# Thirty-two bytes of padding ahead of the weight ring of a two-block transformer kernel

## The chip, the cores and the metric

The kernel runs on one core of one Trainium2 chip. The metric is device time in microseconds of one execution. Three runs of the kernel before took 1617.83, 1611.34 and 1613.09 us; their median is 1613.09 us.

## The reference

One sequence of 256 tokens and 1024 features goes through two blocks, in fp32.

```
first_block:   h += mix(rmsnorm(h)) @ w_out          # 8 forgetting heads, 8 stick-breaking heads
               h += cross_attention(h, mem)          # 4 heads, 256 memory rows
               h += moe(rmsnorm(h))                  # router, 16 experts of 256 hidden units
               x  = rmsnorm(h)
second_block:  for l in 0, 1:                        # also carries 256 context rows through layer 0
                 h = modulate(rmsnorm(x), ...) @ w_in
                 x += gate * (concat(fourier, mLSTM both ways, latent attention) @ w_out)
                 x += gate * (square(relu(modulate(rmsnorm(x)) @ w_up)) @ w_down)   # 4096 hidden
               return rmsnorm(x)
```

Nearly all of the arithmetic is products of an activation matrix of 256 or 512 rows with fp32 weights.

## The kernel before

Activations lie feature-major: a tile such as `res` or `uh` holds, for each block of 128 features, 256 or 512 token columns. Weights come as 350 pieces of [128, 1024] fp32 (`PIECE`), 4,096 bytes in every partition, in the order in which they are used.

The precision of fp32 is kept by splitting each operand in two parts of type fp32r. For each piece SyncE's queue starts a DMA into a slot of `ring` (L471, L479, L483), four slots in turn (`RING`). ScalarE rounds the slot into `wh` (`hi_part`, L600), VectorE writes the remainder into `wl` (`lo_part`, L1747), and TensorE multiplies. ScalarE and VectorE run three pieces ahead (`AHEAD`). A slot of `ring` may be loaded again when VectorE has written the `wl` of its former piece (semaphore `w_lo`); a slot of `wh` and `wl` may be written again when TensorE has begun the next piece (`piece_used`).

A block of 128 weights takes three matmuls, `prod` at L1124 (weights stationary, activations moving) or `prod_t` at L1131 (the other way round); all are issued at L1100:

```
mm(o, h, xh, start=start, stop=False, **flags)
mm(o, h, xl, start=False, stop=False, **flags)
return mm(o, lo, xh, start=False, stop=stop, **flags)
```

So one piece is 24 matmuls. In the names of the profile the moving operand stands first and the stationary one second: `pair<-uh,wh` moves `uh` against the weights `wh`.

The moving pairs are `uh`,`ul` (projections, output products, up products), `xh`,`xl` (queries of the cross attention), `fh`,`fl` and `hidh`,`hidl` (experts), and `hh`,`hl` (down products). In `prod_t` `wh` and `wl` move and `uh` and `ul` are stationary (values of the first block and some of the second).

Places in SBUF are given out by hand. The base is rounded up to 32 bytes and every tile is put at a running count of fp32 words:

```
base = (nc.sbuf_base + 31) // 32 * 32
return nc.alloc_sbuf_tensor_at(name, list(shape), dtype, offset=base + 4 * off)
```

Ahead of the ring `take` gives out, in words: `table` 3,976, `lw` 1,408, `res`, `uh` and `ul` 4,096 each, `sq` and the row buffers 2,560 each, `rstd` 512, `small` 256, `modv` 192, `gmod` 64, `macc` 16, `gcol` 32. That is 23,864 words or 95,456 bytes, 745 times 128 and 96 over. With a base on a multiple of 128 bytes, `table` starts at 0 past such a multiple, `lw` up to `gmod` (`uh`, `ul` and `sq` among them) at 32 past one, and `macc`, `gcol`, `ring`, `wh`, `wl`, `spin` and the common region `w0` at 96 past one. In `w0` lie, one after the other and over each other, `qk`, `kx`, `vx`, `qx`, `xh`/`xl`, `fh`/`fl`, `gates`, `eg`, `hidh`/`hidl`, `qkp`, `qc`, `mv`, `mo`, `va`, `pf`, `cq`, `ya`, `hh`/`hl` and the early buffers `qk_w` and `qk_c`. Their places count from `w0` in multiples of 16 words.

Of the kernel before, what the change touches and what calls it, by code (L numbers as in the profile page):

```python
# [228 lines left out]
def build(nc, w_stream, mod_stream, c_rows, ml_dram, gate_dram, table_in, small_in, x_in, mem_in, ctx_in, out):  # L229
    with ExitStack() as stack:  # L230
# [11 lines left out]
        def at(name, shape, off, dtype=F32):  # L242
            n = int(np.prod(shape[1:]))
            return nc.alloc_sbuf_tensor_at(name, list(shape), dtype, offset=base + 4 * off)

        def take(n):
            top[0] += n
            return top[0] - n
# [23 lines left out]
        gmod = at("gmod", [P, 2 * NL, 16], take(64))  # L272
        macc = at("macc", [P, 2 * UNIT_TURN], take(16))
        gcol = at("gcol", [P, 2, 4, MH], take(32))
        ring = at("ring", [P, RING, PIECE], take(RING * PIECE))
        wh = at("wh", [P, RING, PIECE], take(RING * PIECE), F32R)
        wl = at("wl", [P, RING, PIECE], take(RING * PIECE), F32R)
# [2442 lines left out]
```

## Time and profile before

| | |
|---|---|
| median of three runs | 1613.09 us (1611.34 to 1617.83) |
| span of the profiled execution, first to last instruction | 1611.0 us |
| TensorE, matmuls | 1552.7 us busy, 96% of the span, 9,912 of them |
| VectorE | 1068.4 us busy, 66% |
| ScalarE | 758.7 us busy, 47% |
| mean granted TensorE clock | 0.994 of 2.4 GHz |
| DMA | 254.90 MB, 158 GB/s over the span |

The profile gives the profiled execution's span; its own time is not listed apart from the three runs above. A busy matmul's end is modelled and overlaps the next one's start, so the time that a matmul costs is read from one start to the next, not from its duration.

### The profile page before, as it was taken

To read this page: it belongs to the slowest core of one execution; us is meant where nothing else is said; L and a number is where in the kernel's file an instruction comes from. 1 tells how busy PE (TensorE), PEld (TensorE's weight loads), DVE (VectorE), ACT (ScalarE), POOL (GpSimd) and SP (SyncE) were. 2 spreads that over 40 slices of the span, in tenths; PEclk is the share of its full clock that TensorE was granted. 3 is DMA by queue.
4 is the path that set the end of the run, shared out by engine and by line. 5 is a ranking of instruction groups with operands and counts; after the bars stand their busy time and mean duration, and the time that the engine had idled before them with its cause. 6 is when DMAs were issued, how large, how long until landed. Compare 5 with 4: busy or idle time off the path is not lost.

```text
span 1611.0 us, 27225 instructions
## 1 busy us (share of the span) xinstructions
PE 1552.7 (96%) x9912; PEld 1367.7 (85%) x9912; DVE 1068.4 (66%) x1834; ACT 758.7 (47%) x1302; POOL 99.7 (6%) x167
## 2 busy tenths in 40 slices
PE   7999999999999999998799999999999998999997
PEld 7998798999999987765587888888887875899997
DVE  5877586888888879516856645555577845665554
ACT  5544544544444454434634532245225355574562
POOL 0011000000000000000200100010000002000000
PEclk9999999999999999999999999999999999999999
DMA  8675172677777733320241754455453442245552
GB/s 338 220 273 193 53 240 85 211 244 244 241 242 243 227 92 110 100 66 18 62 131 63 237 179 148 143 184 196 142 161 91 127 110 40 88 153 188 174 182 91
DMA packets 71784, 254.90 MB, mean 158 GB/s; under 512 B 7920, under 2 KB 11152, under 8 KB 71456
## 3 DMA queue, kind: packets, MB, share of 16 engines
q1 hardware_dynamic: 54048, 189.43, 36.1%
q0 software_dynamic: 17664, 64.49, 13.2%
q8 instruction: 48, 0.79, 0.2%
q14 instruction: 24, 0.20, 0.0%
HBM read 252.78 MB, written 1.11 MB: 158 GB/s over the span
## 4 chain that ended last, share of the span: by engine, by line
PE 86%; DVE 8%; ACT 3%; issue 2%; DMA 0%; DVEq 0%; SPq 0%; ACTq 0%
PE pair L1100 85%; PE pair L1144 1%; DVE sq L2359 1%; ACT wh L600 1%; DVE uv L1788 1%; DVE sq L1828 1%; DVE small L1820 1%; PE pair L1289 1%; ACT sq L668 0%; DMA table<-in_table 0%; DVE wl L1747 0%; ACT rstd L637 0%; DVE ul L1777 0%; DVE res L2512 0%; ACT rstd L639 0%
## 5 line engine op out<-in xcount | busy, mean ns | idle before, releaser
L1747 DVE TENSOR_TENSOR wl<-ring,wh 128x1024 fp32r<-128x1024 f32 x350 | 426.4, 1222 | 202.4 <-ACT wh L600 198.3
L600 ACT ACTIVATE wh<-ring 128x1024 fp32r<-128x1024 f32 x350 | 366.6, 1052 | 263.9 <-PE pair L1100 245.9
L1100 PE MATMUL pair<-uh,wh 128*128 128x256 f32 (+3 forms) x1280 | 417.3, 326 | 6.8 <-DVE ul L1779 4.1
L1100 PE MATMUL pair<-uh,wl 128*128 128x256 f32 (+3 forms) x1280 | 413.1, 323 | 0.0
L1100 PE MATMUL pair<-ul,wh 128*128 128x256 f32 (+3 forms) x1280 | 412.0, 322 | 0.0
L1100 PEld LDWEIGHTS pair<-uh,wh 128*128 128x128 f32 (+1 forms) x1280 | 235.8, 184 | 32.9 <-issue 8.2
L1100 PEld LDWEIGHTS pair<-uh,wl 128*128 128x128 f32 (+1 forms) x1280 | 235.9, 184 | 23.9
L1100 PEld LDWEIGHTS pair<-ul,wh 128*128 128x128 f32 (+1 forms) x1280 | 235.7, 184 | 23.3
L1100 PE MATMUL pair<-hh,wh 128*128 128x512 f32 (+1 forms) x512 | 172.7, 337 | 0.8
L1100 PE MATMUL pair<-hh,wl 128*128 128x512 f32 (+1 forms) x512 | 172.0, 336 | 0.0
L1100 PE MATMUL pair<-hl,wh 128*128 128x512 f32 (+1 forms) x512 | 172.0, 336 | 0.0
L1100 PE MATMUL pair<-fh,wh 128*128 128x256 f32 x520 | 147.5, 284 | 1.1 <-DVE res L1975 1.1
L1100 PE MATMUL pair<-fl,wh 128*128 128x256 f32 x520 | 147.1, 283 | 0.0
L1100 PE MATMUL pair<-fh,wl 128*128 128x256 f32 x520 | 147.1, 283 | 0.0
L1100 PEld LDWEIGHTS pair<-hh,wh 128*128 128x128 f32 x512 | 97.1, 190 | 11.9 <-issue 2.0
L1100 PEld LDWEIGHTS pair<-hl,wh 128*128 128x128 f32 x512 | 97.2, 190 | 10.1
L1100 PEld LDWEIGHTS pair<-hh,wl 128*128 128x128 f32 x512 | 97.1, 190 | 10.0
L1100 PEld LDWEIGHTS pair<-fh,wh 128*128 128x128 f32 x520 | 99.8, 192 | 1.3 <-DVE res L1975 1.3
L1100 PEld LDWEIGHTS pair<-fl,wh 128*128 128x128 f32 x520 | 99.8, 192 | 0.0
L1100 PEld LDWEIGHTS pair<-fh,wl 128*128 128x128 f32 x520 | 99.8, 192 | 0.0
L2480 DVE TENSOR_TENSOR hl<-sq,hh 128x512 f32 (+1 forms) x64 | 35.7, 558 | 95.0 <-ACT hh L1059 94.9
L1054 ACT ACTIVATE sq<-pair 128x512 f32<-128x512 f32 (+1 forms) x64 | 31.3, 489 | 107.3 <-PE pair L1100 107.3
(304 smaller groups left out, 2439.3 us busy)
## 6 DMA issues: line engine op xcount, KB each, us to landing
ring<-in_w_stream SPq DMA_DIRECT2D x350, 512.0 KB, 4.2
mod_w<-in_mods POOLq DMA_DIRECT2D x48, 512.0 KB, 3.8
uh_f<-in_mods POOLq DMA_DIRECT2D x42, 512.0 KB, 5.1
qk_w<-in_mods POOLq DMA_DIRECT2D x6, 512.0 KB, 7.0
uv<-c_rows POOLq DMA_DIRECT2D x4, 512.0 KB, 7.0
ml<-ml_dram POOLq DMA_DIRECT2D x4, 512.0 KB, 7.7
table<-in_table SPq DMA_DIRECT2D x1, 1849.5 KB, 12.6
res<-in_x SPq DMA_DIRECT2D x4, 256.0 KB, 4.1
```

Source lines behind the costliest of these rows:

```text
L600: act.activation(wh[:, s, :], ring[:, s, :], ACT.Copy).then_inc(S("w_hi"), 1)
L1054: act.activation(r, bank[(b0 + j) % 4][:, 0:n], ACT.Relu).then_inc(S("job_emptied_act"), 1)
L1100: ins = pe.matmul(*operands, **flags)
L1144: pe.matmul(bank[b], spin[:, 0:P], spin[:, :], start=True, stop=True)
L1289: last = pe.transpose(bank[6][:, to * P:(to + 1) * P], prob[i % 2][:, j * P:(j + 1) * P], ident)
L1747: tt(wl[:, s, :], ring[:, s, :], wh[:, s, :].bitcast(F32), ALU.subtract).then_inc(S("w_lo"), 1)
L1788: last = stt(o, src, g, r, ALU.mult, ALU.mult)
L1820: dve.tensor_reduce(smv(i, 0, 0, g), b, AX_X, ALU.max, negate=True).then_inc(S("sm_max"), 1)
L1828: last = ts(p, p, smv(i, 1, k), None, ALU.mult)
L2359: last = stt(e[:, tc], bank[4 + kb % 2][:, tc], MD ** -0.5, e[:, tc], ALU.mult, ALU.mult)
L2480: tt(hl[:, d, 0:n].rearrange("p a b -> p (a b)"), sq[:, 2 + j % 2, 0:n], hh[:, d, 0:n].rearrange("p a b -> p (a b)").bitcast(F32), ALU.sub ...
```

## The change

One line takes eight words that nothing uses. Everything that is given out after it starts 32 bytes later; nothing else differs: the instructions, their order, their waits and their shapes are the same.

```
         gcol = at("gcol", [P, 2, 4, MH], take(32))
+        take(8)
         ring = at("ring", [P, RING, PIECE], take(RING * PIECE))
         wh = at("wh", [P, RING, PIECE], take(RING * PIECE), F32R)
         wl = at("wl", [P, RING, PIECE], take(RING * PIECE), F32R)
```

With the base as above, `ring`, `wh`, `wl`, `spin` and `w0` then start on a multiple of 128 bytes, and every tile in `w0` on a multiple of 64. `table`, `res`, `uh`, `ul`, `sq` and the others ahead of the line stay where they were.

## Rows read from the trace of the kernel before

**Rows 1.** The page: span, busy time, and the chain that ended last.
```profile
span 1611.0 us, 27225 instructions
PE 1552.7 (96%) x9912; PEld 1367.7 (85%) x9912; DVE 1068.4 (66%) x1834; ACT 758.7 (47%) x1302; POOL 99.7 (6%) x167
...
PE 86%; DVE 8%; ACT 3%; issue 2%; DMA 0%; DVEq 0%; SPq 0%; ACTq 0%
PE pair L1100 85%; PE pair L1144 1%; DVE sq L2359 1%; ACT wh L600 1%; DVE uv L1788 1%; DVE sq L1828 1%; DVE small L1820 1%; PE pair L1289 1%; ACT sq L668 0%; DMA table<-in_table 0%; DVE wl L1747 0%; ACT rstd L637 0%; DVE ul L1777 0%; DVE res L2512 0%; ACT rstd L639 0%
```

**Rows 2.** Groups of TensorE by form: names, shape, count; busy us, mean ns.
```profile
L1100 PE MATMUL pair<-uh,wh 128*128 128x256 f32 x696 | 196.6, 282 | 5.0 <-DVE ul L1779 2.2 <-DVE wl L1747 1.1 <-DVE ul L1777 1.1
...
L1100 PE MATMUL pair<-uh,wh 128*128 128x512 f32 x392 | 155.2, 396 | 1.9 <-DVE ul L1779 1.9
...
L1100 PE MATMUL pair<-fh,wh 128*128 128x256 f32 x520 | 147.5, 284 | 1.1 <-DVE res L1975 1.1
...
L1100 PE MATMUL pair<-hh,wh 128*128 128x512 f32 x256 | 99.6, 389 | 0.0
...
L1100 PE MATMUL pair<-hh,wh 128*128 128x256 f32 x256 | 73.0, 285 | 0.8
L1100 PE MATMUL pair<-hidh,wh 128*128 128x256 f32 x256 | 72.4, 283 | 0.0
...
L1100 PE MATMUL pair<-wh,uh 128*128 128x256 f32 x128 | 35.4, 277 | 0.0
```

**Rows 3.** The chain in four stretches without a wait: start us, us, matmuls.
```profile
68.99 21.08 PE pair L1100 x186
...
305.95 259.08 PE pair L1100 x2159
...
864.77 80.34 PE pair L1100 x351
...
954.96 80.24 PE pair L1100 x354
```

**Rows 4.** TensorE's timeline, two stretches: start us, us; first and last rows.
```profile
142.81 0.28 PE L1100 MATMUL pair<-wh,uh 128*128 128x256 f32 x1
...
143.98 0.28 PE L1100 MATMUL pair<-wl,uh 128*128 128x256 f32 x1
...
263.76 0.28 PE L1100 MATMUL pair<-uh,wh 128*128 128x256 f32 x1
...
266.12 0.28 PE L1100 MATMUL pair<-uh,wl 128*128 128x256 f32 x1
```

**Rows 5.** Who waited for whom: us in total, times, longest us.
```profile
ACT wh L600 <- PE pair L1100: 245.9, 113, 4.5
...
ACT wh L600 <- DMA ring<-in_w_stream: 17.8, 13, 3.3
...
PE pair L1100 <- DMA table<-in_table: 8.5, 1, 8.5
...
PE pair L1100 <- DVE wl L1747: 1.1, 2, 0.7
```

**Rows 6.** The tile `ring`: time of its DMAs from issue to landing.
```profile
DMA to landing us min/median/max: 3.4/4.2/10.6
```

**Rows 7.** Groups of VectorE and ScalarE by form: names, shapes, count; busy us, mean ns.
```profile
L1747 DVE TENSOR_TENSOR wl<-ring,wh 128x1024 fp32r<-128x1024 f32 x350 | 426.4, 1222 | 202.4 <-ACT wh L600 198.3 <-issue 3.3 <-DVE sq L2494 0.4
...
L1880 DVE CUSTOM_DVE_ANT_1 uh_f<-uh_f,uv 128x1024 f32<-128x1024 f32 x12 | 14.6, 1220 | 0.0
...
L1880 DVE CUSTOM_DVE_ANT_0 qk_w<-qk_w,qk_c 128x1024 f32<-128x1024 f32 x6 | 7.3, 1214 | 0.0
...
L2273 DVE SCALAR_TENSOR_TENSOR qc<-qkp,table,qc 96x256 f32<-96x256 f32 x16 | 7.7, 481 | 0.6
...
L1788 DVE SCALAR_TENSOR_TENSOR uv<-res,gmod,rstd 128x256 f32<-128x256 f32 x40 | 17.3, 477 | 3.8 <-ACT rstd L639 3.8
...
L600 ACT ACTIVATE wh<-ring 128x1024 fp32r<-128x1024 f32 x350 | 366.6, 1052 | 263.9 <-PE pair L1100 245.9 <-DMA ring<-in_w_stream 17.8
```

More of the change, by code:

```diff
@@ L274, in build @@
         gcol = at("gcol", [P, 2, 4, MH], take(32))
+        take(8)
         ring = at("ring", [P, RING, PIECE], take(RING * PIECE))
```

## The prediction

> **What bounds the kernel now.** I read the page first. TensorE's matmuls fill 1552.7 of 1611.0 us, and the chain that ended last runs through TensorE for 86% of the span, through VectorE for 8%, ScalarE for 3% and DMA for 0% [rows 1]. The reader should see two things there: the time is made by matmuls that follow each other without a wait, and weight loading is not on the path. The waits say the same. ScalarE's rounding of weights waited 245.9 us for TensorE and only 17.8 us for the ring's DMAs, and TensorE waited 1.1 us in all for VectorE's remainder of a piece [rows 5].
>
> So the first question of a change of addresses is whether the pace of the matmuls depends on an address. A matmul's duration in the groups (282 ns for 256 columns) overlaps the next one [rows 2], so I took the pace from unbroken stretches of the chain [rows 3] and from starts in the timeline [rows 4]:
>
> - `fh`,`fl` and `hidh`,`hidl` moving, 256 columns: 259.08 us for 2,159, or 120.0 ns each.
> - `uh`,`ul` moving, 256 columns: 20 steps from 263.76 to 266.12, or 118.0 ns.
> - `wh`,`wl` moving, `uh`,`ul` stationary, 256 columns: 21.08 us for 186, or 113.3 ns, in one stretch; 10 steps from 142.81 to 143.98, or 117 ns, in another.
> - `uh`,`ul` moving, 512 columns: 80.34 us for 351, or 228.9 ns.
> - `hh`,`hl` moving, 512 columns: 80.24 us for 354, or 226.7 ns.
>
> From 256 to 512 columns of operands behind the ring the pace grows by 226.7 - 120.0 = 106.7 ns, so the columns alone cost 106.7 ns per 256, and what lies on top is 6.7 ns (113.3), 11.3 ns (118.0) or 13.3 ns (120.0 and 226.7). These differ with the operands, and the operands differ in their place modulo 128: `uh` and `ul` at 32, everything behind the ring at 96. That is all that speaks for an effect. Against it: the same operands with the same form ran at 113.3 and at 117 ns in two stretches, at one and the same alignment. So at least part of the spread is a rhythm into which TensorE's loads and matmuls fall, not an alignment.
>
> **The change part by part.** No instruction, wait or DMA is added, removed or reordered. Four things could still cost differently.
>
> *The ring's DMAs.* 350 of them now write 32 bytes further on. A landing takes 4.2 us in the median [rows 6]. ScalarE works three pieces ahead, and a piece is 24 matmuls: 24 x 118.0 ns = 2.8 us, three are 8.5 us. A landing could take twice as long before TensorE saw it in the steady stretches. Where it doesn't hide, at the start, TensorE's longest DMA wait is for `table` (8.5 us), which does not move, and its waits for a split piece are 1.1 us [rows 5]. Bounds -1.1 and +1.1 us; I take 0.
>
> *ScalarE and VectorE.* `wl` from `ring` and `wh`, 1,024 elements at 96 past a multiple of 128, takes 1222 ns. A pass of the same size over tiles at 32 past one takes 1220 ns (`uh_f`), one over tiles at 96 takes 1214 ns (`qk_w`). The convolution reads `qkp` shifted by single words and takes 481 ns for 256 elements, against 477 ns for the unshifted `uv` [rows 7]. So a shift by four bytes costs at most 4 ns, 0.8%. These two engines hold 11% of the chain, 177 us [rows 1]; 0.8% of it is 1.4 us. Bounds -1.4 and +1.4 us; I take 0. The rest of their work is covered by TensorE: a piece costs VectorE 1222 ns and ScalarE 1052 ns [rows 7] against its 2.8 us there.
>
> *Matmuls whose two operands both move by 32 bytes.* These are `fh`,`fl` (520 each of three), `hidh`,`hidl` (256 each) and `hh`,`hl` at 256 columns (256 each): 3 x 1,032 = 3,096; and 3 x 256 = 768 of 512 columns [rows 2]. Their distance to each other stays, the place modulo 128 changes. No fp32r operand of the trace starts on a multiple of 64, so this is bounded. Lowest: nothing but the columns, 3,096 x 13.3 ns + 768 x 13.3 ns = 41.2 + 10.2 = 51.4 us saved. Highest: one more step of the size seen between 113.3 and 120.0, 6.7 ns on each: 3,864 x 6.7 ns = 25.9 us lost. I take 0, because the nearest rows, the pair at 113.3 and 117 ns at one alignment, show paces that change without it.
>
> *Matmuls of which one operand moves.* `uh`,`ul` against `wh`,`wl`: 3 x 696 = 2,088 of 256 columns, 3 x 392 = 1,176 of 512; and 3 x 128 = 384 with `wh`,`wl` moving [rows 2]. Lowest: all of 256 columns at 113.3, 2,088 x 4.7 ns = 9.8 us saved, and 1,176 x 6.7 ns = 7.9 us. Highest: 2,088 x 2.0 ns (to 120.0) + 1,176 x 6.7 ns + 384 x 6.7 ns (113.3 to 120.0) = 4.2 + 7.9 + 2.6 = 14.7 us lost. I take 0 for the same reason.
>
> The Trainium skill (Advanced Engine Details and Errata, Memory Cachelines) puts SBUF's lines at 16 bytes; 96 and 0 past a multiple of 128 are both starts of such a line, and by this rule no operand would gain or lose. It leaves the three paces unexplained, and no run here shows the size of a line.
>
> The sum is 0 on a span of 1611.0 us. The profiled execution's own time isn't listed apart; its span lies just under the fastest of the three runs (1611.34) and 2.1 us below their median of 1613.09, so I forecast 1612 us, between the two.
>
> **The rivals.**
>
> *Faster: alignment sets the extra time of a matmul (chance 0.33).* For it: operands behind the ring hold 120.0 ns over 2,159 matmuls without one slip, those at 32 hold 118.0, as if the place fixed the step; and the steps between paces are 6.7 ns, the time of 16 columns or 64 bytes, which is what a start off a multiple of 64 could cost. Against it: the two paces at one alignment. If operands that both move fall one step: 3,864 x 6.7 ns = 25.9 us, 1587 us. If the `uh` matmuls of 256 columns follow to 113.3, 9.8 us more, 1577 us. If half of the first comes, 1600 us.
>
> *Slower: the distance between `uh` and the weights decides (chance 0.21).* `uh` at 32 and `wh` at 96 were 64 bytes apart modulo 128 and become 32 apart; should weight load and moving read then meet more often, only the matmuls with one moved operand pay: 14.7 us as above, 1628 us (1620 to 1635). It decides from about 2.3 ns on each of the 3,648. For it: `uh` against `wh` is quicker than `fh` against `wh` (118.0 to 120.0), so something in the pairing counts. Against it: at 512 columns the order is the other way round (228.9 to 226.7).
>
> *The change doesn't do what it says (0.03, inside no change).* The base is only rounded to 32 bytes; if it isn't on a multiple of 128, neither is the ring after the change. That would be another place modulo 128, with the same forecast.
>
> *A quicker DMA is hidden (inside no change).* If the landings became shorter, ScalarE's 17.8 us of waiting would shrink, and the chain, which has 0% of DMA, would not.
>
> **How the numbers follow.** No change (within 0.5%, or 8 us, about what a measurement of this kernel tells from none): 0.46; faster 0.33; slower 0.21. The likeliest is 1612 us, its own range 1605 to 1620. The range for 8 in 10 takes in the one-step gain (1587) with little to spare and most of the slower case: 1585 to 1627. It leaves out the gain with `uh` following and the far end of the slower case.
>
> **What would show it.** Right: the same paces in the same stretches, 120.0 ns for `fh`, 118.0 for `uh`, 228.9 and 226.7 ns for 512 columns, `wl` at 1222 ns and `wh` at 1052 ns, landings near 4.2 us. Wrong: the stretch of 2,159 matmuls of the experts, 259.08 us long, shortens to about 245 us (113.3 ns) or lengthens; or the stretch of 351 of `uh` with 512 columns leaves 80.34 us. If the span changes and all paces stand, the cause lies in the waits between stretches, and I would have missed it.

## The result and the profile after

The changed kernel takes 1618.07 us (median of 20 runs, 1614.44 to 1621.77) against 1614.32 us (20 runs) before. The ratio is 1.0023 with a 95% interval of 1.0012 to 1.0034: 3.7 us slower, small but clear of noise. The forecast of 1612 us stood for no change, a little below the time before, and the time rose; the slower rival had named the place and overpriced it.

The page after (compare [rows 1]). TensorE's busy time grew by 8.5 us, VectorE's and ScalarE's did not, and the chain runs through TensorE as before:

```profile
span 1619.3 us, 27225 instructions
PE 1561.2 (96%) x9912; PEld 1370.4 (85%) x9912; DVE 1068.2 (66%) x1834; ACT 758.2 (47%) x1302; POOL 99.7 (6%) x167
...
PE 87%; DVE 7%; ACT 3%; issue 2%; DMA 0%; DVEq 0%; SPq 0%; ACTq 0%
```

ScalarE's and VectorE's split of a piece and the ring's landings (compare [rows 5 to 7]). The source's lines are one higher in number now. The groups, busy us and mean ns:

```profile
L1748 DVE TENSOR_TENSOR wl<-ring,wh 128x1024 fp32r<-128x1024 f32 x350 | 426.5, 1223 | 202.8 <-ACT wh L601 198.7
L601 ACT ACTIVATE wh<-ring 128x1024 fp32r<-128x1024 f32 x350 | 366.5, 1052 | 259.2 <-PE pair L1101 245.4
```

and the tile `ring`:

```profile
DMA to landing us min/median/max: 3.3/4.2/11.5
```

1223 against 1222 ns, 1052 against 1052, 4.2 us against 4.2: these three steps held. The chain's stretches (start us, us, matmuls; compare [rows 3], in the order of the stages) show what moved:

```profile
68.94 21.06 PE pair L1101 x178
...
263.95 16.10 PE pair L1101 x138
...
307.90 259.20 PE pair L1101 x2160
...
869.85 80.27 PE pair L1101 x344
...
959.87 80.24 PE pair L1101 x354
```

The reader divides. `fh` and `hidh` moving: 259.20 / 2,160 = 120.0 ns, as before. `hh` with 512 columns: 80.24 / 354 = 226.7 ns, as before. `uh` with 512 columns: 80.27 / 344 = 233.3 ns, where it was 228.9. `wh` moving against `uh`: 21.06 / 178 = 118.3 ns, where it was 113.3. `uh` with 256 columns: 16.10 / 138 = 116.7 ns, where the same stretch before (16.14 us for 137) had 117.8. Only pairs of which one operand moved have another pace.

The steps from one matmul's start to the next, averaged over all of a kind in the trace (steps over 1.12 times the median, which hold a wait, left out), give the sum:

| moving, stationary, columns | matmuls | before ns | after ns | us |
|---|---|---|---|---|
| `uh`, weights, 512 | 1,176 | 229.06 | 233.31 | +5.0 |
| `uh`, weights, 256 | 2,088 | 117.52 | 117.13 | -0.8 |
| weights, `uh`, 256 | 384 | 114.05 | 118.35 | +1.7 |
| weights, `uh`, 384 | 192 | 175.69 | 173.42 | -0.4 |
| `uh`, 96 weights, 512 and 256 | 288 each | 233.30, 113.92 | 231.71, 116.71 | +0.3 |
| `fh`, `hidh`, `xh`, `hh` | 4,056 | | within 0.1 | -0.1 |
| sum | | | | +5.7 |

The 20 runs of each kernel differ by 3.7 us, the steps by 5.7. The two profiled spans differ by 8.3 us. Most of the rest of that is the clock: the profile after has two more stretches at the 1.2 GHz level. In windows of TensorE (busy us, matmuls, granted clock, DMA share, GB/s) after:

```profile
170.00:189.00 19.00, 17.82 (x104) 1.00 0.00 1
190.00:194.00 4.00, 4.00 (x16) 0.57 0.00 0
...
787.00:791.00 4.00, 4.00 (x16) 0.59 0.08 26
```

and before in the first of these places:

```profile
190.00:194.00 4.00, 4.00 (x30) 1.00 0.00 0
```

16 matmuls in place of 30, 14 x 0.12 us = 1.6 us in the first. In the second, the same work, from 14 matmuls `mv`,`sq` to the next group but one of the same pair, took from 783.29 to 787.36 us before and from 785.78 to 791.52 us after: 4.07 and 5.74 us, 1.7 us more. With the steps' 5.7 us that is 9.0 us, 0.7 more than the spans say. The 19 us ahead of the first stretch held a TensorE busy for 17.82 us with 104 matmuls. The same window before held 17.46 us with 102, and the clock there stayed up, so these rows don't tell why it fell. Nor do the runs make the clock a trait of the change: the 20 runs of the changed kernel have a mean granted clock of 0.9946, the 35 runs of the kernel before that were timed beside the first four experiments 0.9937. At a mean granted clock of 0.998 the changed kernel took 1614.4 and 1614.8 us, at 0.992 1620.0 to 1621.8, about 1.1 us for a thousandth.

### The profile page after: what moved, and what is told of

The parts are those of the page before. It is cut to its first block, busy times and chain, and to the rows that moved or that the text cites. A ratio compares the mean times of both kernels' runs of the same rounds, so it can differ in the third digit from the quotient of the medians.

```text
span 1619.3 us, 27225 instructions
## 1 busy us (share of the span) xinstructions
PE 1561.2 (96%) x9912; PEld 1370.4 (85%) x9912; DVE 1068.2 (66%) x1834; ACT 758.2 (47%) x1302; POOL 99.7 (6%) x167
## 4 chain that ended last, share of the span: by engine, by line
PE 87%; DVE 7%; ACT 3%; issue 2%; DMA 0%; DVEq 0%; SPq 0%; ACTq 0%
PE pair L1101 85%; PE pair L1145 1%; DVE sq L2360 1%; ACT wh L601 1%; DVE uv L1789 1%; DVE sq L1829 1%; DVE small L1821 1%; PE pair L1290 1%; ACT sq L669 0%; DVE wl L1748 0%; DMA table<-in_table 0%; ACT rstd L638 0%; DVE ul L1778 0%; DVE res L2513 0%; ACT rstd L640 0%
## 5 line engine op out<-in xcount | busy, mean ns | idle before, releaser
L1748 DVE TENSOR_TENSOR wl<-ring,wh 128x1024 fp32r<-128x1024 f32 x350 | 426.5, 1223 | 202.8 <-ACT wh L601 198.7
L601 ACT ACTIVATE wh<-ring 128x1024 fp32r<-128x1024 f32 x350 | 366.5, 1052 | 259.2 <-PE pair L1101 245.4
```

Source lines behind the costliest of these rows:

```text
L601: act.activation(wh[:, s, :], ring[:, s, :], ACT.Copy).then_inc(S("w_hi"), 1)
L1748: tt(wl[:, s, :], ring[:, s, :], wh[:, s, :].bitcast(F32), ALU.subtract).then_inc(S("w_lo"), 1)
```

## The experiments

Write d for the start of the moving operand less the start of the stationary one, modulo 256 bytes. Before, `uh` on weights has d = 64, the pairs behind the ring have 0, and weights on `uh` have 192. The change makes these 32, 0 and 224. Theory after the result: d sets the pace. Main rival: the operand's own place modulo 128 does. A distance doesn't depend on the base from which all places count, so the prediction's worry about the base has no part in what follows.

**Everything 32 bytes later.** No padding at the ring:

```
+        take(8)
         table = at("table", [P, N_COLS], take((N_COLS + 7) // 8 * 8))
```

> Eight words are taken ahead of the first tile and none ahead of the ring: every tile starts 32 bytes later, the distance between any two tiles is that of the kernel before. Theory (distance between moving and stationary operand modulo 128 sets the pace): paces as before, uh moving 512 columns 229 ns, uh moving 256 columns 117.8 ns, wh moving 256 columns 113 ns, fh 120.0 ns; time within 0.1% of before. Rival A (the operand's own place modulo 128 sets the pace): weights on a multiple of 128 as in the changed kernel, so 233.3 ns for uh with 512 columns and 118.3 ns for wh moving; time about 0.2% over before.

Measured: ratio 0.9999 (0.9983 to 1.0016). The weights now lie where the changed kernel has them, and the pace of `uh` with 512 columns is that of before, 76.22 / 333 = 228.9 ns:

```profile
869.88 76.22 PE pair L1101 x333
```

`fh` stays at 120.0 and `uh` with 256 columns at 117.5 ns. Weights and `uh` have both changed their place modulo 128 and their pace is that of before, so the operand's own place falls as a cause. One detail missed: the first stretch of `wh` moving, 192 matmuls, ran at 117.8 instead of 113.4 ns; with it the mean of that kind is 116.3, not 113.

**Sixteen words instead of eight, d = 0 everywhere.**

```
+        take(16)
         ring = at("ring", [P, RING, PIECE], take(RING * PIECE))
```

> Sixteen words ahead of the ring in place of eight: ring, wh, wl and all behind start at 32 past a multiple of 128, as uh and ul do, so moving and stationary operand are at distance 0 in every matmul, as they are for fh, hidh and hh in all kernels. Theory (distance): all fp32r pairs pace as those do, 120.0 ns for 256 and 226.7 ns for 512 columns. uh with 256 columns 2,088 x +2.2 ns = +4.6 us, uh with 512 columns 1,176 x -2.3 ns = -2.7 us, wh moving 256 columns 384 x +6.6 ns = +2.5 us: in all +4 us or +0.3% over before. Rival A (own place): weights at 32 are a new place, fh and hh would leave 120.0 and 226.7 ns. Rival B (no address matters, the paces are chance): paces of before or of after come back in no order.

Measured: 1.0017 (1.0002 to 1.0032), +2.7 us where +4 were expected. `uh` with 512 columns, then `wh` moving:

```profile
867.97 80.24 PE pair L1101 x354
...
69.91 18.12 PE pair L1101 x151
```

80.24 / 354 = 226.7 and 18.12 / 151 = 120.0 ns, and `uh` with 256 columns 119.9: at d = 0 `uh` paces exactly as `fh` and `hh` do. `fh` and `hh` kept theirs, so both rivals fall: weights at a new place changed nothing for them, and the paces came in the order of d.

**Thirty-two words, the same place modulo 128.** The diff is the same with `take(32)`.

> Thirty-two words ahead of the ring: ring and all behind start 128 bytes later than before, the same place modulo 128. Theory (distance modulo 128): paces and time as before, uh 512 columns 229 ns, wh moving 256 columns 113 ns, time within 0.1% of before. Rival C (the period is 256 bytes or more, or any move of the addresses reshuffles the paces): at least one of these paces moves by 1 ns or more.

Measured: 1.0006 (0.9988 to 1.0024). The time stands, the paces don't: `uh` with 512 columns

```profile
863.81 80.27 PE pair L1101 x344
```

goes to 233.3 ns and with 256 columns to 115.2. So the period is not 128 bytes. `uh` is at d = 192 here, at 64 before. The two shifts cancel (+5.0 and -4.8 us), which is why a time alone would have said "no effect". That any move reshuffles the paces is ruled out by the first experiment.

**Only the region behind the weights 32 bytes later.**

```
+        take(8)
         w0 = take(16464)
```

> Eight words are taken ahead of the region w0 alone: ring, wh and wl stay at 96 as before, fh, hidh, xh and hh move to 0, 32 bytes ahead of the weights. Theory (distance): uh pairs stay at 229, 117.8 and 113 ns; the pairs with fh, hidh, xh and hh leave 120.0 and 226.7 ns, which no change so far has moved: if +32 does what the change did to uh at -32 bytes (or the reverse), 256 columns go to 116.7 to 118 ns and 512 columns to 229 to 233 ns: 3,288 x -2 to -3.3 ns = -6.6 to -10.9 us and 768 x +2.3 to +6.6 ns = +1.8 to +5.1 us, in all -9 to -1.5 us. Rival D (only uh and ul, ahead of the ring, are sensitive): fh and hh stay at 120.0 and 226.7 ns, time as before.

Measured: 0.9976 (0.9959 to 0.9994), -3.9 us. The first line is `fh` and `hidh`, the second `hh` with 512 columns:

```profile
309.96 240.10 PE pair L1101 x2058
...
949.91 70.23 PE pair L1101 x301
```

116.7 and 233.3 ns: the two paces that `uh` took in the changed kernel, at the same d = 32. The rival that only `uh` is sensitive falls.

These kernels also show that 256 bytes is a period. Counted modulo 512, `uh` starts 256 bytes past the weights in the kernel with sixteen words and `fh` and `hh` start level with them, and all pace alike (120.0 and 226.7 ns). `uh` is at 288 in the changed kernel and `fh` and `hh` at 32 here, and again both show 116.7 and 233.3 ns. Steps finer than 32 bytes were not tried.

**The other distances.** Four kernels with words ahead of the ring and ahead of `w0`: 48 and 32, 24 and 48, 40 and 40, 56 and 24.

> Forty-eight words ahead of the ring and thirty-two ahead of w0: uh to wh is 128 bytes modulo 256, and fh, hidh, xh, hh to wh is 128 bytes modulo 256 as well. Theory with period 128: distance 0 modulo 128 everywhere, so 120.0 ns for 256 and 226.7 ns for 512 columns for all pairs, as with sixteen words ahead of the ring; time +0.2 to +0.3% over before. Theory with period 256: a distance not seen yet, at least one of the two paces differs by 1 ns or more.

> Twenty-four words ahead of the ring and forty-eight ahead of w0: wh lies 32 bytes (modulo 128) above uh, and fh, hidh, xh, hh lie 64 bytes (modulo 128) from wh. Theory (distance modulo 128, sign indifferent): uh pairs pace as in the changed kernel, 116.7 and 233.3 ns; fh and hidh go from 120.0 to the two paces seen at 64, 113.3 or 117.8 ns, hh with 512 columns from 226.7 to 229.0 or 233.3 ns. Time: fh, hidh, xh, hh 256 columns 3,288 x -2.2 to -6.7 ns = -7 to -22 us, hh 512 columns +2 to +5 us, uh as the changed kernel +4 us: -1 to -14 us against before. Rival D (fh and hh keep what 32 bytes gave, 116.8 and 233.3 ns, at any distance but 0): 116.8 ns at 64 too.

> Forty words ahead of the ring and forty ahead of w0: uh is 96 bytes modulo 256 from wh, and fh, hidh, xh, hh 160 bytes. Theory with period 128 and sign indifferent: all pairs are 32 bytes from the weights, 116.7 ns and 233.3 ns for all. With period 256: uh or fh, at least one, paces otherwise.

> Fifty-six words ahead of the ring and twenty-four ahead of w0: uh is 160 bytes modulo 256 from wh, fh, hidh, xh, hh 96 bytes from it in the same direction as in the kernel with forty words, mirrored. Theory with period 128 and sign indifferent: the same paces as there, 116.7 ns and 233.3 ns for all pairs, and a time within 0.15% of that kernel's. If the sign counts: the paces of uh and of fh change places between the two kernels.

Measured, in that order: 1.0051 (1.0030 to 1.0072), 0.9969 (0.9952 to 0.9986), 1.0057 (1.0042 to 1.0072), 1.0092 (1.0066 to 1.0118). The chain of `fh` and `hidh` in the four, in the same order:

```profile
314.93 245.17 PE pair L1102 x2066
```
```profile
309.99 240.04 PE pair L1102 x2118
```
```profile
314.95 245.11 PE pair L1102 x2089
```
```profile
319.90 240.12 PE pair L1102 x2001
```

118.7, 113.3, 117.3 and 120.0 ns. Period 128 is refuted (120.0 was expected at 128 and 118.7 came), so is the rival that `fh` has one pace at every distance but 0 (113.3 at 192, where 32 gave 116.7), and so is an indifferent sign (32 gives 116.7, 224 gives 118.3). The last expectation was badly framed: it took the distances of `uh` and `fh` as mirrored, but by the signed d both are at 160 in the kernel with 40 words and both at 96 in the one with 56, and so they did not change places; both went from 117.4 and 118.3 to 119.9. Sorted by d, all kinds of the ten kernels so far fall together: they agree within 0.2 ns where a distance has one pace, and within 2.5 ns where the mean mixes two (weights of 128 columns; mean step in ns, each from the trace of a kernel that has that d):

| d | 256: `uh` | 256: `fh` | 256: `wh` on `uh` | 512: `uh` | 512: `hh` |
|---|---|---|---|---|---|
| 0 | 119.9 | 120.0 | 119.9 | 226.9 | 226.8 |
| 32 | 117.1 | 116.8 | 116.7 | 233.3 | 233.3 |
| 64 | 117.5 | | 115.0 | 229.1 | |
| 96 | 119.9 | 119.9 | 120.0 | 233.3 | 233.3 |
| 128 | 119.2 | 118.7 | 119.0 | 232.5 | 232.4 |
| 160 | 118.3 | 117.4 | 118.0 | 234.3 | 234.3 |
| 192 | 115.2 | 113.4 | 114.1 | 233.3 | 233.3 |
| 224 | 118.3 | | 118.4 | 233.3 | |

The means at 256 columns are mixtures wherever the kinds disagree: a stretch runs at one of two levels and mostly keeps it from its first few matmuls to its end. The levels are 113.3 and 117.8 ns at 64 and 192, 116.7 and 117.8 at 32, 118.7 and 120.0 at 128, 117.3 and 118.7 at 160. At 0 and 96 (120.0) and at 224 (118.3) only one was seen. The changed kernel shows both levels of d = 32: the stretch of `uh` at 263.95 us above has 116.7 ns, and this later one has 28.15 / 239 = 117.8:

```profile
1436.88 28.15 PE pair L1101 x239
```

Weights of 96 columns follow another order: with 512 columns of `uh` moving they take 233.3 ns at 64, 230.0 at 0 and 228.5 at 192. So the table holds for weights of 128 columns alone.

A rival that the table leaves open is that TensorE's reads meet those of VectorE and ScalarE, which work on `ring`, `wh` and `wl` at the same time, and these tiles share one place modulo 256. The traces speak against it. Before, the steps of `fh` average 120.0 ns both where VectorE and ScalarE were busy throughout (576 steps) and where both were idle (306). After, those of `uh` with 512 columns average 233.5 ns (148 steps) and 233.2 ns (146).

The sum of the steps of all kinds against before is +0.5, +3.8, -0.7, -4.4, +10.7, -6.9, +8.8 and +16.7 us for the eight kernels in the order told; the ratios say -0.2, +2.7, +1.0, -3.9, +8.2, -5.0, +9.2 and +14.8.

**Placing each operand.** The table says what to do: 192 for 256 columns, 0 for 512.

```
-        xh = at("xh", [P, KT, T], w0 + 2048, F32R)
+        xh = at("xh", [P, KT, T], w0 + 2048 + 48, F32R)
...
-        fh = at("fh", [P, KT, T], w0 + 8192, F32R)
+        fh = at("fh", [P, KT, T], w0 + 8192 - 16, F32R)
...
-        hidh = at("hidh", [P, 2, T], w0 + 4608, F32R)
+        hidh = at("hidh", [P, 2, T], w0 + 4608 + 48, F32R)
...
-        hh = at("hh", [P, MC, 512], w0, F32R)
+        hh_of = [at("hh", [P, MC, 512], w0, F32R), at("hh1", [P, MC, 512], w0 + 48, F32R)]
```

`xl`, `xv`, `fl`, `fv`, `hidl` and `hl` go with their partners, and the MLP uses `hh_of[l]` and `hl_of[l]`.

> The ring stays where it was. Each moving operand behind it gets the place that the runs so far showed to be quickest for its shape: fh, fl, hidh, hidl, xh, xl and a second name for hh, hl in layer 1 (256 columns) lie 192 bytes modulo 256 above wh (fh by -64 bytes, the others by +192), hh and hl in layer 0 (512 columns) stay at 0. Theory (moving start minus stationary start, modulo 256, sets the pace): fh and hidh 113.3 ns, 2,328 x -6.6 ns = -15.4 us; xh 113.3 or 117.8 ns, -0.4 to -1.3 us; hh with 256 columns 113.3 to 117.8 ns, -1.6 to -5.0 us; hh with 512 columns stays at 226.7 ns, uh as before: in all -17 to -22 us, 1591 to 1596 us against 1613. Rival E (each of these tiles was quick only because the whole region had moved, or the gain comes back as waits for VectorE's split, whose cover per piece shrinks from 2.88 to 2.72 us): less than half of it, 1604 us or more.

Measured: 1595.61 us, 0.989 (0.9862 to 0.9917), -17.7 us; the steps sum to -19.4. The chain, first `fh` and `hidh`, then `hh` with 512 columns:

```profile
309.91 230.18 PE pair L1100 x2031
...
941.87 78.20 PE pair L1100 x345
```

and TensorE's waits for the split (us, times, longest):

```profile
PE pair L1100 <- DVE wl L1747: 1.3, 3, 0.7
```

113.3 and 226.7 ns. TensorE's waits for VectorE's split are 1.3 us against 1.1, so nothing was given back. `fh` lies 64 bytes lower here and `hidh` 192 bytes higher, 256 bytes apart by distance, and both have 113.3 ns: the period once more. Most of the gain, 15.2 us, comes from `fh` and `hidh`, and it hangs on the long stretch of the experts taking the lower of its two levels: at 117.8 ns the same 2,328 matmuls would have saved 5.1 us (2,328 x 2.2 ns). It took the lower one in all three kernels with `fh` at 192, but no run shows why.

**The same with `uh` at 192 as well**, by `take(32)` ahead of the ring.

> As the kernel with placed operands, with the ring and all behind it 128 bytes later, so that uh and ul too lie at 192 modulo 256 above the weights. Theory: uh with 256 columns at 113.3 or 117.8 ns (115.2 on average when this was done alone), -4.9 us, uh with 512 columns from 229.0 to 233.3 ns, +5.0 us, 96 columns wide -0.7 us: within 3 us of the kernel with placed operands and the old ring. Rival (the two levels at 192 settle at 113.3 once the others do): uh with 256 columns 113.4 ns throughout, 4 us less.

Measured: 1591.91 us, 0.9884 (0.9852 to 0.9915), the lowest median of the study. `uh` with 256 columns means 114.1 ns, nearer the lower level than alone (115.2), with 512 columns 233.3:

```profile
845.96 79.10 PE pair L1101 x339
```

The two medians differ by 3.7 us, the ratios by 1.0 us, which lies within both intervals; the steps say 4.1 us. The rival's 113.4 ns throughout did not come.

**One of three weights apart.** `take(16)` ahead of `wl`, `take(48)` ahead of `w0`: of the matmuls with `fh` only the one on `wl` is at 192. The edit moves `wl` away from `uh` too, so every other kind also gets two distances.

> Sixteen words between wh and wl and forty-eight ahead of w0: fh and wh stay at 0 modulo 256, fh against wl is at 192, so one of three matmuls has another distance. The order is (wh, fh), (wh, fl), (wl, fh). Theory H1 (a matmul's own stationary operand counts): the step from the third matmul's start to the next shortens, the other two stay at 120.0. Theory H2 (the load that runs beside the moving read counts, the next matmul's weights): the step of the second matmul shortens, during which wl is loaded, the other two stay. Either gives about 117.8 ns on average over fh (two at 120.0 and one at 113.3); a mean outside 117 to 119 ns speaks for a rhythm over all three in which neither holds alone.

Measured in one run (1612.99 us): the steps after (wh, fh), (wh, fl) and (wl, fh) are 117.6, 117.5 and 118.4 ns. The timeline of TensorE shows them nearly even:

```profile
399.76 0.28 PE L1102 MATMUL pair<-fh,wh 128*128 128x256 f32 x1
399.88 0.28 PE L1102 MATMUL pair<-fl,wh 128*128 128x256 f32 x1
399.99 0.28 PE L1102 MATMUL pair<-fh,wl 128*128 128x256 f32 x1
400.11 0.28 PE L1102 MATMUL pair<-fh,wh 128*128 128x256 f32 x1
```

The mean, 117.8 ns, is the expected one; the split isn't. All three steps shortened, so neither the matmul's own weights nor the load beside it can be named. The mean is weak evidence too, as 117.8 ns is also the upper level at 192. The other kinds show that the three do not simply add: `hh` with 512 columns has 231.1 ns, where two steps of 226.7 and one of 233.3 would give 228.9. That speaks for a rhythm over all three.

## Why the prediction was wrong, step by step

- *TensorE's chain is the time, so the pace is the question*: right. Every kernel's time followed the sum of its steps to within 3 us (4.8 for the one with `uh` at 192 as well).
- *The ring's DMAs, ScalarE and VectorE cost 0*: right, by the lines above.
- *Both operands moved: 0*: right (-0.1 us), but not for the reason given, that paces change without an alignment. They kept their pace because their distance stays. The sum left out the 192 matmuls of `xh`,`xl`, which didn't change either. The bounds (-51.4, +25.9 us) came from absolute place, which the first experiment refutes.
- *One operand moved: 0*: this is the step that failed. The sum is +5.8 us: 512 columns +5.0 (bound 7.9), 256 columns -0.8 (bound +4.2), `wh` moving +1.7 (bound 2.6), the 384 columns and the narrow weights, which I left out, -0.1. I took 0 because one pair ran at 113.3 and at 117 ns at one alignment [rows 3, 4]. That observation was sound and the inference wasn't: at 64 and 192 there are two levels, but which set of levels exists depends on the distance. Two causes in one number don't exclude each other. The list of what lies on top of the columns also passed over the row that moved most: `uh` with 512 columns had 228.9 - 213.4 = 15.5 ns on top, which fits none of the three sizes named, and it went to 20.0.
- *The time inside its likeliest range (1605 to 1620 us)*: luck. Three kinds left their pace, and the time stayed near because the shifts are small and partly cancel.
- *Slower rival, distance decides*: the mechanism that the runs showed. Its price, 14.7 us, was the upper bound of each row, with the sign of the 256 columns wrong; and it took the period for 128 bytes, where 256 was found. Its objection (at 512 columns the order is reversed) is no objection: 256 and 512 columns have different orders over d.
- *Faster rival, alignment to 64 or 128 bytes*: refuted by moving everything.
- *The rule of the Trainium skill (Advanced Engine Details and Errata, Memory Cachelines) on lines of 16 bytes*: it left 0 and 96 alike. The runs show an effect of steps of 32 bytes, all of them starts of such lines, so this rule doesn't account for it, and no run here shows the size of a line.

## What to carry to other kernels

Where matmuls with separate fp32r weight loads are back to back, the pace can depend on where the moving operand starts relative to the weights; read it from starts, not from durations, and per shape. Padding that "aligns" one buffer changes its distance to all others: move everything once and one tile once, and compare. When paces of opposite sign are at work, an unchanged time doesn't show that nothing changed.

## What the runs showed of the hardware that was not expected

- The step of an fp32r matmul with its weight load of 128 columns depends on d modulo 256 bytes, the same for four kinds of moving operand: 113.3 to 120.0 ns for 256 columns, 226.7 to 234.3 for 512. Moving all tiles by 32 bytes changes none of these distances, and the time stands (0.9999).
- 226.7 - 120.0 = 106.7 ns is 256 columns at 2.4 GHz; what lies on top is 6.7 ns (113.3), 13.3 ns (120.0 and 226.7) or 20.0 ns (233.3) at the commonest levels, multiples of the time of 16 columns. Others, such as 116.7, 117.3 and 118.3 ns, lie between.
- At 32, 64, 128, 160 and 192 two levels exist for the same operands, farthest apart at 64 and 192 (113.3, 117.8 ns). What picks one at the start of a stretch stays open, as does what in TensorE's reads and loads makes the distance count.
